# A hybrid decoder trunk: the input projection by 128 columns at a time, its side products in two banks

## The reference, cut to what matters

```python
h = layer_norm(concat([meta, x]))                      # 272 tokens, 2048 features
for l in range(2):
    u, fq, fk, fv, ff, dq, ckv, iq, ik, iw = split(h @ w_in[l])
    y_ssm = s5(u, ...)                                 # diagonal state space, 64 groups of 16, gated
    y_fox = attention(fq, fk, fv, forget(ff))
    dk, dv = split(rms_norm(ckv) @ w_kv_up[l])         # latents
    dq, dk, iq, ik = rope(dq), rope(dk), rope(iq), rope(ik)   # rotations
    y_dsa = sparse_attention(dq, dk, dv, top_k(iq, ik, iw))
    h = layer_norm(ALPHA * h + concat(norms(y_ssm, y_fox, y_dsa)) @ w_out[l])
    h = layer_norm(ALPHA * h + (silu(gate) * val) @ w_down[l])  # val, gate: causal conv of h @ w_up
```

## Time and profile before

| | us |
|---|---|
| median of 3 runs (lowest, highest) | 2754.89 (2753.76, 2758.51) |
| the profiled execution | 2759.53 |
| its span, first to last instruction | 2757.7 |
| PE busy | 2605.1 (94%) |
| DVE busy | 1778.7 (65%) |
| ACT busy | 1378.2 (50%) |
| steps of layer 0, first `chunk_sums` to the end | 73 to 311 |
| steps of layer 1 | 1447 to 1687 |

### The profile page before, as it was taken

One profiled execution on the slowest core, in us unless ns is written; L12 is line 12 of the kernel. 1 busy time (PEld: TensorE's weight loads), 2 busy tenths in 40 slices (PEclk: granted clock), 3 DMA queues, 4 the chain that ended last, 5 costly groups with the idle time before them and its releaser, 6 DMA issues.

```text
span 2757.7 us, 55922 instructions
## 1 busy us (share of the span) xinstructions
PE 2605.1 (94%) x21738; PEld 2495.7 (90%) x21738; DVE 1778.7 (65%) x2778; ACT 1378.2 (50%) x2097; POOL 11.9 (0%) x19
## 2 busy tenths in 40 slices
PE   5989999979999999999979899999799999999997
PEld 5988778879999999999979787888799999999997
DVE  6876576676666666544488765666766666665445
ACT  5443465455555555433354444654566666653334
POOL 0000000000000000000000000000000000000000
PEclk8999999989999999999999999999899999999999
DMA  4433122335555555555444331223355555555553
GB/s 167 149 103 109 62 100 92 118 109 172 181 172 170 175 180 174 173 174 169 163 147 146 100 108 62 100 85 130 108 182 182 183 182 182 182 182 185 174 186 109
DMA packets 109732, 401.91 MB, mean 146 GB/s; under 512 B 12176, under 2 KB 12176, under 8 KB 109584
## 3 DMA queue, kind: packets, MB, share of 16 engines
q1 hardware_dynamic: 108432, 395.15, 43.5%
q0 software_dynamic: 1152, 4.63, 0.4%
HBM read 397.50 MB, written 2.23 MB: 145 GB/s over the span
## 4 chain that ended last, share of the span: by engine, by line
PE 89%; DVE 6%; ACT 2%; issue 2%; DMA 1%; SPq 0%; ACTq 0%; DVEq 0%
PE ps L407 26%; PE ps L408 25%; PE ps L409 25%; PE ps L645 2%; PE ps L632 1%; PE ps L481 1%; PE ps L611 1%; PE ps L587 1%; PE ps L580 1%; PE ps L490 1%; DVE h L1153 1%; ACT h L772 1%; PE ps L495 1%; DVE h L1133 1%; DMA raw<-stream 1%
## 5 line engine op out<-in xcount | busy, mean ns | idle before, releaser
L756 ACT ACTIVATE w_hi<-raw 128x1024 fp32r<-128x1024 f32 x728 | 763.2, 1056 | 830.7 <-PE ps L409 808.4
L408 PE MATMUL ps<-x_lo,w_hi 128*128 128x272 f32 (+1 forms) x3904 | 1124.8, 288 | 0.0
L409 PE MATMUL ps<-x_hi,w_hi 128*128 128x272 f32 (+1 forms) x3904 | 1123.0, 288 | 0.0
L1078 DVE TENSOR_TENSOR w_lo<-raw,w_hi 128x1024 fp32r<-128x1024 f32 x528 | 638.8, 1224 | 542.2 <-ACT w_hi L756 542.1
L407 PE MATMUL ps<-x_hi,w_lo 128*128 128x272 f32 (+1 forms) x2816 | 805.6, 286 | 18.8 <-DVE x_lo L1161 18.4
L408 PEld LDWEIGHTS ps<-x_lo,w_hi 128*128 128x128 f32 x3904 | 744.1, 191 | 1.6
L409 PEld LDWEIGHTS ps<-x_hi,w_hi 128*128 128x128 f32 x3904 | 743.9, 191 | 0.0
L407 PEld LDWEIGHTS ps<-x_hi,w_lo 128*128 128x128 f32 x2816 | 531.0, 189 | 20.5 <-issue 18.0
L407 PE MATMUL ps<-g_hi,w_lo 128*128 128x272 f32 (+1 forms) x1408 | 403.0, 286 | 4.5 <-issue 4.5
L408 PE MATMUL ps<-g_lo,w_hi 128*128 128x272 f32 (+1 forms) x1408 | 402.4, 286 | 0.0
L409 PE MATMUL ps<-g_hi,w_hi 128*128 128x272 f32 (+1 forms) x1408 | 400.8, 285 | 0.0
(11 more groups left out here) (262 smaller groups left out, 2952.8 us busy)
## 6 DMA issues: line engine op xcount, KB each, us to landing
raw<-stream SPq DMA_DIRECT2D x744, 512.0 KB, 3.4
h<-x SPq DMA_DIRECT2D x4, 544.0 KB, 6.0
out<-h SPq DMA_DIRECT2D x4, 544.0 KB, 2.7
cst<-consts POOLq DMA_DIRECT2D x2, 724.0 KB, 6.3
wkv<-w_kv POOLq DMA_DIRECT2D x2, 512.0 KB, 7.7
b_st<-ssm_b POOLq DMA_DIRECT2D x2, 512.0 KB, 9.2
c_st<-ssm_c POOLq DMA_DIRECT2D x2, 512.0 KB, 11.2
par<-params SPq DMA_DIRECT2D x1, 562.0 KB, 11.9
```

Source lines behind the costliest of these rows:

```text
L408: pe.matmul(acc, w_hi[:, slot, kk, cols], lo, start=False, stop=False)
L409: mm = pe.matmul(acc, w_hi[:, slot, kk, cols], hi, start=False, stop=k == tiles - 1)
L756: act.activation(w_hi[:, slot, :, :], raw[:, slot, :, :], ACT.Copy).then_inc(hi_made, 1)
L1078: dve.tensor_tensor(w_low(phase, slot), raw[:, slot, :, :], w_hi[:, slot, :, :].bitcast(F32), ALU.subtract).then_inc(in_lo_made if phase = ...
```

## The change

The stream's blocks of the input projection are cut another way: a block now holds 8 feature tiles for 128 columns, two blocks make a column tile, and a tile fills one bank. The first four tiles (`WIDE`) are interleaved, so that the first four blocks of a layer are the first halves (k 0 to 7) of tiles 0 to 3 in banks 0 to 3, and the next four the second halves. Later tiles follow one after another in banks 0 and 1 by turns. ACT reads each tile by itself (`read_tile`, 30 a layer, instead of 15 pairs) and counts them in a semaphore of their own, `in_read`; PE waits for the tile two before. The low parts of the first four blocks are made at other turns of the norm's loop.

Banks 2 and 3 are then free during the steps. All side products alternate between them in their order `SIDE`, and each waits only for the reader of the one two before. The waits of `chunk_sums` for side products and those of side products for `p_read` go. Two value transposes swap banks 3 and 7.

```diff
+WIDE = 4
+IN_ORDER = [(t, b) for b in range(2) for t in range(WIDE)] + [(t, b) for t in range(WIDE, TILES_IN) for b in range(2)]
+SIDE = [("rope", 0), ("ms", 0)] + [("rope", r) for r in range(1, 9)] + [("kv", t) for t in range(8)] + [("rope", r) for r in range(9, 13)]
+def side_bank(kind, n):
+    return 2 + SIDE.index((kind, n)) % 2
-V_BANKS = (4, 5, 3, 0, 1, 7)
+V_BANKS = (4, 5, 7, 0, 1, 3)
...
@@ chunk_sums
-                step = 2 * m + 1
-                made = [r for s in range(step) for r in ROPE_STEPS.get(s, ())] + list(ROPE_STEPS.get(step, ()))[0:1]
-                if made:
-                    pe.wait_ge(roped, l * ROPES + max(made) + 1)
-                if step > MS_STEP:
-                    pe.wait_ge(ckv_sd, l + 1)
-                done = [t for s in range(step) for t in KV_STEPS.get(s, ())] + list(KV_STEPS.get(step, ()))[0:1]
-                if done:
-                    pe.wait_ge(kv_made, l * 8 + max(done) + 1)
...
@@ in_blocks
-                    if b == 0:
-                        pe.wait_ge(psum_free, first_group(l, "in") + g + 1)
+                    if b == 0 and t < WIDE:
+                        pe.wait_ge(psum_free, first_group(l, "glu") + 2)
+                    elif b == 0:
+                        pe.wait_ge(in_read, l * TILES_IN + (t - 1 if t >= WIDE + 2 else t - WIDE + 1))
                     pe.wait_ge(in_lo_made, first_low(l, "in") + n + 1)
-                    split_block("in", (first_block(l, "in") + n) % SLOTS, b, 2 * (g % 2), DT, x_parts,
-                                (lambda k: (xlo_made, CHUNKS * 2 * l + k // 2 + 1)) if g == 0 else None)
+                    acc = ps[:, t if t < WIDE else t % 2, 0:NT]
+                    for kk in range(2 * KB):
+                        k = 2 * KB * b + kk
+                        if t < WIDE and k % 2 == 0:
+                            pe.wait_ge(xlo_made, CHUNKS * 2 * l + k // 2 + 1)
+                        pe.matmul(acc, lo_w[:, kk, :], x_hi[:, k, :], start=k == 0, stop=False)
+                        pe.matmul(acc, hi_w[:, kk, :], x_lo[:, k, :], start=False, stop=False)
+                        mm = pe.matmul(acc, hi_w[:, kk, :], x_hi[:, k, :], start=False, stop=k == DT - 1)
+            def side_free(l, kind, n):
+                at = SIDE.index((kind, n)) - 2
+                if at < 0:
+                    return
+                before, i = SIDE[at]
+                if before == "rope":
+                    pe.wait_ge(roped, l * ROPES + i + 1)
+                elif before == "ms":
+                    pe.wait_ge(ckv_sd, l + 1)
+                else:
+                    pe.wait_ge(kv_made, l * 8 + i + 1)
...
@@ side_products
-                    if r == 1:
-                        pe.wait_ge(ckv_sd, l + 1)
-                    elif r == 9:
-                        pe.wait_ge(kv_made, 8 * (l + 1))
-                    pe.wait_ge(p_read, l * UT + sums_before(step, half))
-                    if l * ROPES + r and r < 12:
-                        pe.wait_ge(roped, l * ROPES + r)
+                    side_free(l, "rope", r)
+                    if r >= 9:
+                        pe.wait_ge(kv_made, l * 8 + r - 8)
...
@@ ACT: read_group becomes read_tile
-                        for n in blocks_at(step, i):
-                            if n % 4 == 3:
-                                read_group(n // 4)
+                        for n in blocks_at(step, i):
+                            if IN_ORDER[n][1]:
+                                read_tile(n)
...
@@ DVE: layer_norm
+                late_lows = (1, 4, 5, 6) if n == 0 else (3, 5) if low_parts and low_parts[1] == "up" else (4, 6)
-                    if low_parts and c in ((3, 5) if n else (1, 3, 5, 7)):
-                        low_part(*low_parts, c // 2 + (1 if n else 0))
+                    if low_parts and c in late_lows:
+                        low_part(*low_parts, 4 - len(late_lows) + late_lows.index(c))
```

More of the change, by code:

```diff
@@ L54 @@
 BLOCKS_PER_LAYER = sum(g * b for g, b, _ in PHASES.values())
-GROUPS_PER_LAYER = sum(g for g, _, _ in PHASES.values())
+GROUPS_PER_LAYER = sum(g for p, (g, _, _) in PHASES.items() if p != "in")
 SPLIT_PER_LAYER = sum(PHASES[p][0] * PHASES[p][1] for p in SPLIT)
@@ L86 @@
 PW = CH + 1
-GROUPS_IN = PHASES["in"][0]
-BLOCKS_IN = 4 * GROUPS_IN
+TILES_IN = 2 * PHASES["in"][0]
+BLOCKS_IN = 2 * TILES_IN
+WIDE = 4
+IN_ORDER = [(t, b) for b in range(2) for t in range(WIDE)] + [(t, b) for t in range(WIDE, TILES_IN) for b in range(2)]
 STEPS = 2 * UT + 1
@@ L95, in blocks_at, with tiles_before @@
     return [n] if n < BLOCKS_IN and not (step % 2 and pos == 3) else []
-def groups_before(step):
-    return max(0, (4 + 7 * (step // 2) + 4 * (step % 2)) // 4)
+def tiles_before(step):
+    n = 4 + 7 * (step // 2) + 4 * (step % 2)
+    return sum(b for _, b in IN_ORDER[0:max(n, 0)])
 ROPE_STEPS = {6: (0,), 7: (1, 2), 8: (3, 4), 9: (5, 6), 10: (7, 8), 15: (9, 10), 16: (11, 12)}
@@ L143 @@
 PARAM_COLS = _at
-def sums_before(step, half):
-    return min(UT, step // 2 + (half if step % 2 else 0))
 def hybrid_trunk(nc, x, stream, consts, params, ssm_b, ssm_c, w_kv, out):
@@ L669, in _ @@
                     m = step // 2
-                    pe.wait_ge(psum_free, first_group(l, "in") + groups_before(step - 1) + 2)
+                    pe.wait_ge(in_read, l * TILES_IN + tiles_before(step - 1))
                     side_products(l, step, 0)
@@ L799, in _, with read_tile @@
                 act.activation(flat[3], flat[1], ACT.Sin, bias=HALF_PI, scale=-TWO_PI_LOW).then_inc(trig_made, 1)
[L801 to L809, removed]
+                def read_tile(n):
+                    t = IN_ORDER[n][0]
+                    bank = t if t < WIDE else t % 2
+                    act.wait_ge(block_used, first_block(l, "in") + n + 1)
+                    dst, src = proj[:, t, :], ps[:, bank, 0:NT]
+                    if t < U0 + UT:
+                        dst = dst.rearrange("p (r j) -> p r j", r=CH)
+                        src = src.rearrange("p (j r) -> p r j", r=CH)
+                    if t == FFIW:
                         for half in range(2):
-                            act.activation(proj[64 * half:64 * half + 64, IK, :], ps[64:P, bank + 1, 0:NT], ACT.Copy)
-                    act.activation(dst, src, ACT.Copy, scale=SCALE if FQ0 <= 2 * g < FQ0 + 4 else 1.0).then_inc(psum_free, 1)
+                            act.activation(proj[64 * half:64 * half + 64, IK, :], ps[64:P, bank, 0:NT], ACT.Copy)
+                    act.activation(dst, src, ACT.Copy, scale=SCALE if FQ0 <= t < FQ0 + 4 else 1.0).then_inc(in_read, 1)
                 def wave_table(m):
@@ L846, in read_outputs @@
                                    ACT.Copy).then_inc(y_read, 1)
-                cast(l, "in", 5)
-                cast(l, "in", 6)
-                read_group(0)
-                cast(l, "in", 7)
+                for n in range(5, 8):
+                    cast(l, "in", n)
                 for step in range(STEPS):
@@ L855, in _ @@
                         act.wait_ge(ckv_ms, l + 1)
-                        act.activation(rstd[:, :], ps[:, 7, 0:NT], ACT.Sqrt, bias=RMS_EPS, scale=1.0 / KV_RANK).then_inc(ckv_sd, 1)
+                        act.activation(rstd[:, :], ps[:, side_bank("ms", 0), 0:NT], ACT.Sqrt, bias=RMS_EPS, scale=1.0 / KV_RANK).then_inc(ckv_sd, 1)
                     if step == GATE_STEP:
@@ L867, in _ @@
                             act.wait_ge(kv_mm, l * 8 + t + 1)
-                            act.activation(kv[:, t, :], ps[:, 7, 0:NT], ACT.Copy).then_inc(kv_made, 1)
+                            act.activation(kv[:, t, :], ps[:, side_bank("kv", t), 0:NT], ACT.Copy).then_inc(kv_made, 1)
                         if i == 2 and step % 2 == 0 and 1 <= m <= UT:
@@ L1694, in blocks_of, with tile_blocks @@
     return w.reshape(k // (KB * P), KB, P, m // (2 * P), 2 * P).transpose(3, 0, 2, 1, 4).reshape(-1, P, KB * 2 * P)
+def tile_blocks(w):
+    k, m = w.shape
+    a = w.reshape(2, 2 * KB, P, m // P, P).transpose(3, 0, 2, 1, 4).reshape(m // P, 2, P, KB * 2 * P)
+    return np.stack([a[t, b] for t, b in IN_ORDER])
 def constants():
```

40 lines of the change are left out of this document (19 added, 21 removed).

## The result

The changed kernel takes 2716.21 us (median of 4, 2715.41 to 2717.05) against 2756.23 (median of 4, 2753.76 to 2758.51) for the kernel before: a ratio of 0.9854, 95% interval 0.9842 to 0.9867, 40.0 us less. The forecast was 2712, with 2700 to 2729 as its range. The profiled execution's span fell from 2757.7 to 2713.6 us, by 44.1; the forecast for it was 2714.7.

A forecast was written before the change was run, and what follows sets the result against it. PE was taken as the bound, 94% busy. Terms: -50.7 for removed stalls, +6.2 new waits, +1.7 half clock, -0.2 layer start, together -43.0 us; from the median 2754.9 that gives 2711.9, say 2712, range 2700 to 2729.

The forecast's parts named there:

- What bounds the kernel, and the side products: PE bounds the kernel; its stalls at side products (rotations 1, 3, 7 and short ones) go, gross 50.7 us.
- The three clean lengths: Windows between `chunk_sums` without the long stalls: 28.6 us with three side products, 29.3 with four.
- A third of it is clock: About a third of the gross 50.7 us comes from PE's half clock after the stalls.
- What is late next: In steps 7 to 9 DVE's chain moves 5.1 us forward and no more, so PE waits for it.
- The new waits: 0.6 us at `chunk_sums`(4) and 2.5 us at `chunk_kernel`(4): 3.1 us a layer, 6.2 in all.
- The half clock behind the new wait: After the 2.5 us wait, one half-clock period in the two layers, 1.7 us; bounds 0 and 3.4.
- The start of a layer: Nothing won by the new block order, since DVE's and ACT's chain after the norm sets it; sum -0.2 us.
- The cover of 3.5 us: At a layer's start, waits of 2.05 us for a low part and 1.48 for `abp` absorb slower PE work.
- DVE as the bound of several windows: Rival: DVE becomes the bound of steps 7 to 10, 2720 to 2731 us; chance 0.20.
- The slower one: Rival: 24 matmuls in a row into one bank hold each other up, 2770 us at 20 ns each; chance 0.05.
- the last sentence of the sum: The profiled execution was 4.6 us above the median; this difference carries over, so 2754.9 - 43.0 = 2711.9 us.
- the first rival: DVE becomes the bound of steps 7 to 10, with more half clock or a cold start: 2720 to 2731 us; chance 0.20.

The follow-up runs named there:

- tiles_only: The changed kernel with its new blocks, tiles and start order, but all side products back in bank 7 with the old waits: 2755.6 us, ratio 0.9992 to the kernel before.
- one_back: The changed kernel with each side product waiting for the one just before it, banks still alternating: 2754.87 us, ratio 0.9993 to the kernel before.
- gate12: The changed kernel with the forget gate's work on DVE and ACT in step 12 instead of step 8: 2705.88 us, in a second series 2703.33.
- before_filled: The kernel before with matmuls nobody reads ahead of the waits of rotations 1, 3 and 7: 2743.47 us against 2757.5 beside it, ratio 0.9946.
- wide1: The changed kernel with one column tile interleaved with the norm instead of four: 2716.44 us, ratio 0.9861 to the kernel before.
- wide2: The changed kernel with two column tiles interleaved with the norm instead of four: 2714.73 us, ratio 0.9855 to the kernel before.
- lows35: The changed kernel with the low parts of blocks 2 and 3 before layer 1 at their old turns, 3 and 5: single time 2719.11 us.

## Why the prediction was right, point by point

**What bounds the kernel, and the side products.** Right, and shown by two runs from both sides: tiles_only has all but the side products' waits and gains nothing, one_back has all but the depth of two and gains nothing. The three clean lengths were worked out as 28.6, 29.3 and 29.3; they are 28.66, 29.13 and 29.13 (gate12, where nothing disturbs them). The 0.2 us that 29.3 was too long is 0.2 us more gain in each of the two latent windows (0.8 instead of 0.6), and rotation 11 gave 1.7 instead of 1.3.

**A third of it is clock.** Right in kind, a little high in size. 1.7, 3.0 and 2.6 us were read from two windows at 0.51 and one at 0.95; before_filled gave 1.5, 2.7 and 2.4 back in layer 0, and 2.8, 2.7 and 2.5 in layer 1. That is 14.6 of the 52.9 us by which gate12's windows, with no stall and no dip, and its end of the steps are shorter than those before: 0.28, where the prediction's terms come to 16.0 of 50.7, or 0.32.

**What is late next.** Right in place and size. DVE's timeline of the changed kernel shows the chain that was said to move by 5 us and no more; it begins at 167.28 after ACT's cast, and was to begin 5.1 us ahead of 171.50, at 166.4, counted without the 0.7 us by which this execution's first `chunk_sums` are later:

```profile
167.28 1.23 DVE L1090 TENSOR_TENSOR in_lo_b<-raw,w_hi 128x1024 fp32r<-128x1024 f32 x1 [1.49 <-ACT w_hi L769]
...
179.64 1.38 DVE L1245 TENSOR_TENSOR abp<-terms 64x512 f32<-64x512 f32 x2
...
192.61 0.72 DVE L1289 TENSOR_TENSOR rot<-ps,table 128x544 f32<-128x544 f32 x1
193.25 0.71 DVE L1290 TENSOR_TENSOR rot<-ps,table 128x544 f32<-128x544 f32 x1
```

The new waits were to be 0.6 and 2.5 us; they are 0.38 and 2.42. gate12 adds what the prediction left open, that of all that is done there the gate (on DVE and ACT) was what made DVE late.

**The half clock behind the new wait.** Mis-sized in a small way. One such stretch was charged in the two layers, at 1.7 us. The profiled execution had two, at 1.5 and 1.4 (33.14 and 32.98 against 31.6 without). The same gap of 2.4 us was followed by half clock in both layers of wide1 (33.13, 33.15), in neither of wide2 (31.60, 31.62) and in one of lows35 (33.17, 31.62), so one was a fair middle and no value was to be had from the trace before. Nor did its gap of 2.05 us without half clock behind it tell much: in before_filled the same gap, 2.07 us, was followed by 3.4 us of half clock.

**The start of a layer.** Right: nothing was won, and +0.27 and -0.40 us were measured for +0.2 and -0.4. The rule of the Trainium skill that was weighed against the change ("TensorE: Matmul & The Clock Gate", "A second HAM failure mode: psum-queue depth-cycling": a walk through PSUM banks makes PE idle in small pieces and its clock swing) did not bite: in the window from 73.69, with twice the hand-overs, PE is busy 27.22 of 27.22 us at clock 1.00. The cover of 3.5 us that the sum relied on holds: even a start in which 72 matmuls stand behind the norm's second half (wide1) makes the first `chunk_sums` no later, though in layer 0 it uses the cover up.

**The rivals.** DVE as the bound of several windows didn't come; it bounds one place in one window. The slower one, matmuls held up by 24 additions to one bank, is excluded by tiles_only and by the spacing in the new loop, 0.12 to 0.13 us within a triple and from one to the next, all one bank now:

```profile
80.13 0.29 PE L514 MATMUL ps<-x_hi,w_hi 128*128 128x272 f32 x1
80.25 0.29 PE L512 MATMUL ps<-x_hi,in_lo_b 128*128 128x272 f32 x1
80.38 0.29 PE L513 MATMUL ps<-x_lo,w_hi 128*128 128x272 f32 x1
80.50 0.28 PE L514 MATMUL ps<-x_hi,w_hi 128*128 128x272 f32 x1
```

**The number.** For the profiled execution the sum was -43.0 and the result -44.1, with each term near its measure: gross -50.7 for -52.9, new waits 6.2 for 5.6, their half clock 1.7 for 2.9, a layer's start -0.2 for -0.1. Against the medians the result is -40.0, and 2712 was 4.2 us too low. What failed is the last sentence of the sum, that the profiled execution's distance from the median carries over. It was 4.6 us above the median that the prediction had before (3.3 above the one measured with the result) and 0.8 below it after.

Where the execution before was slow is in part to be seen. Behind the wait of 3.00 us at rotation 1 it ran at half clock in both layers, which made the windows 33.38 and 34.68 us; in tiles_only the same wait had no half clock behind it in either layer (31.88 and 31.88), in one_back in one of the two (34.64 and 31.92). The prediction took both stretches as a sure gain, 1.7 and 3.1 us, where up to 4.3 us were what this one execution had happened to get. That this is what lifted it above the median is not shown, since there is one trace of that kernel.

The rest of the program doesn't account for the difference. Outside the steps the two traces agree to 0.1 us in most stretches. From the end of layer 1's steps to the sums of the norm behind its output projection the changed kernel takes 268.4 us instead of 266.1, with half-clock stretches of 6.8 us where the kernel before has 3.4, but in the stretch behind that 780.4 instead of 782.9, and the two cancel. Such stretches fall differently from one execution to the next: gate12 and gate12_again are one kernel, and take 264.6 and 266.3 us from the end of layer 1's steps to those sums. They are a few us that a difference of two profiles can't know. What decides where they fall stays open.

The upper end of the range, 2729, was called the middle of the first rival; the middle of its 2720 to 2731 is 2725.5. Nothing hangs on it here.

## What to carry to other kernels

Small products that share an accumulator bank with their own successor cost PE here a whole reading by another engine where two of them met in its order; a second bank, waited for two back, removed it. The stall is to be priced with the half-clock stretch behind it, here a bit over a quarter of the whole, and a stretch seen in one execution is no sure one. Then look at what the engine behind the stall was doing meanwhile: it is late next, and a piece of its work that can go to a later step (here one constant) is worth as much as a small rewrite. A restructuring of the big loop can be worth doing for the banks that it frees, even where by itself it brings nothing.

## What the runs showed of the hardware

A wait of 2.4 us of PE at one and the same place was followed by 3.4 us at 1.2 GHz in five of eight layers (changed kernel, wide1, wide2, lows35), at a price of 1.4 to 1.5 us each, and not in the others. A wait of 3.0 us at one place was followed by none, 3.4 or 6.8 us at 1.2 GHz (before, tiles_only, one_back: none in three of six layers). At a layer's start, where PE waits for DVE anyway, raising the clock brought nothing: first products at 0.12 us apart instead of 0.23 moved the first `chunk_sums` by 0.01 us.
